# Up products of the ConvFFN: row block outside, column groups inside

## The chip, the cores and the metric

One core of a Trainium2 chip runs the whole program. The metric is device microseconds of one launch, from the first to the last of its work; a number is the median of several runs unless it is said to come from the profiled execution. TensorE is written PE in the rows (its weight loads PEld), VectorE is DVE, ScalarE is ACT, GpSimd is POOL and the queue that issues most transfers is SP.

## The reference, cut to what matters

The kernel does one step of a two-layer decoder for 1024 prompt rows and 64 sample rows. Each layer has a token mixer and a memory attention in parallel, an output projection, and then a gated feed-forward with a causal width-3 convolution. Only the last part concerns the change:

```python
def conv_ffn(x, gain, w_up, cw, cb, w_down, past_rows):
    T = x.shape[1]
    up = rms_norm(x, gain) @ w_up
    ext = jnp.concatenate([past_rows, up], axis=1)
    conv = cb + sum(cw[j] * ext[:, j:j + T] for j in range(CONV_W))
    out = (jax.nn.silu(conv[..., :D_FF]) * conv[..., D_FF:]) @ w_down
    return out, ext[:, ext.shape[1] - (CONV_W - 1):]
```

D_MODEL is 1024, D_FF is 2816, so `w_up` is 1024 x 5632 and `w_down` 2816 x 1024, for each of two layers.

## The kernel before, in words

Every float32 operand of a large product is held as two parts, a high and a low one (`ff_hi`, `ff_lo` for the activations, `w_hi`, `w_lo` for the weights), and a product is three matmuls into the same PSUM tile: high by high, high by low, low by high. The helper `mm3` issues them at lines 360, 361 and 362, so the rows of the profile carry these three lines wherever a product is made; `mm2` (lines 369 and 370) does the same with two matmuls for the 64 sample rows. One call of `matmul` shows as two records, a weight load of the stationary operand and the matmul that streams the moving one.

The feed-forward of a layer is 22 units, one for each 128 columns of the up projection's first half together with the 128 columns of its gate half. `pe_up` makes the up products of unit u. It has two halves (h = 0 and h = 1). In each, the stationary operand is a 128 x 128 block of `w_hi` or `w_lo`, one for each of 8 row blocks k (KT = 8), and the moving operand is a group of token columns of `ff_hi` or `ff_lo`: three groups of 368, 368 and 352 columns (`TG`, numbered g = 0, 1, 2), each with a PSUM bank of its own: banks 0 to 2 for h = 0, banks 3 to 5 for h = 1. The groups stand outside and the row blocks inside, so 24 matmuls in a row go to one bank. For h = 0 the order of groups is 2, 0, 1, for h = 1 it is 0, 1, 2.

`pe_down` then makes the down products of the unit before (u - 1): 18 outputs of up to 128 x 512, numbered q, that rotate over the banks 6, 7, 0, 1 (`DN_BANK`). VectorE adds each to the residual (`dve_adds`, line 2108 for the prompt rows, lines 2112 and 2116 for the sample rows) and counts them on the semaphore `dn_ev`. Banks 0 and 1 are thus used by the up products and by the down products in turn. Before the up products of u may write banks 0 and 1, the additions up to q = 15 of unit u - 2 must be done; that is the wait on `dn_ev` in `pe_up`, which stands ahead of group 0 and therefore behind the 24 matmuls of group 2 (bank 2 is no bank of `DN_BANK`). The first two units of a layer have nothing to wait for there.

ScalarE waits for a whole half (`up_mm`, then `w_used`) and then empties its three banks; VectorE does the convolution taps, the gate and the split of the gated values. The last unit of a layer (`pe_last`) makes its second half's groups one after the other and tells ScalarE after the second of them (`up_part`). It also makes the down products of two units together; there the moving operands are `d_hi`, `d_lo` and, for the second of them, `d_hi_l`, `d_lo_l` elsewhere in memory.

TensorE works through its program in order: up(0), up(1), down(0), up(2), down(1), and so on.

Of the kernel before, what the change touches and what calls it, by code (L numbers as in the profile page):

```python
# [26 lines left out]
P = 128  # L27
D = 1024
KT = D // P
# [21 lines left out]
TG = [368, 368, 352]  # L51
T0 = [0, 368, 736]
CB = 3
DC = 4
# [15 lines left out]
def build(nc, A, O, scratch):  # L70
    es = ExitStack()
    with es:
# [3 lines left out]
        def sb_at(name, shape, off, dt=F32):  # L76
            return nc.alloc_sbuf_tensor_at(name, shape, dt, offset=off)

        def size(shape):
            n = 4  # L80
            for s in shape[1:]:
                n *= s
            return (n + 31) // 32 * 32

        def sb(name, shape, dt=F32):
            t = sb_at(name, shape, place[0], dt)
            place[0] += size(shape)
            return t
# [20 lines left out]
        ff_hi = sb_at("ff_hi", [P, KT, NTOK + NS], act_hi_at, F32R)  # L109
        ff_lo = sb_at("ff_lo", [P, KT, NTOK], act_hi_at + size([P, KT, NTOK + NS]), F32R)  # L110
        w_hi_at = place[0]
        w_hi = sb("w_hi", [P, 2, KT, UW], F32R)
        w_lo = sb("w_lo", [P, 2, KT, UW], F32R)
# [153 lines left out]
        ps = es.enter_context(nc.psum_tensor("ps", [P, 8, 512], F32))  # L267

        def sem(name):
            return es.enter_context(nc.semaphore(name))  # L270
# [30 lines left out]
        up_mm, up_ev, cv_ok, silu_ok, gate_ok, gh_ok, g_ok, dr_ld, dh_ok, d_ok, dn_mm, dn_ev = (  # L301
            sem(n) for n in ("up_mm", "up_ev", "cv_ok", "silu_ok", "gate_ok", "gh_ok", "g_ok", "dr_ld",
                             "dh_ok", "d_ok", "dn_mm", "dn_ev"))
# [4 lines left out]
        tap_ok, up_part, part_ev, part_ok, part_g, part_h, part_lo = (  # L308
            sem(n) for n in ("tap_ok", "up_part", "part_ev", "part_ok", "part_g", "part_h", "part_lo"))
# [48 lines left out]
        def mm3(pe, out, ahi, alo, bhi, blo, first, last, **kw):  # L358

            pe.matmul(out, ahi, bhi, start=first, stop=False, **kw)  # L360
            pe.matmul(out, ahi, blo, start=False, stop=False, **kw)  # L361
            return pe.matmul(out, alo, bhi, start=False, stop=last, **kw)  # L362
# [1533 lines left out]
        def wpar(l, par):  # L1896
            return (ffn0[l] + par) % 2

        def pe_up(pe, l, u, par, last=False):
            n = u + ffn0[l]  # L1900
            U = u + NFT * l
            pe.wait_ge(w_ok, n + 1)
            w = wpar(l, par)
            for h in range(2):
                if not (isinstance(u, int) and u == 0):

                    pe.wait_ge(up_ev, U * 2 + (h - 1))
                for g in ((0, 1, 2) if h else (2, 0, 1)):
                    if h == 0 and g == 0 and not (isinstance(u, int) and u < 2):

                        pe.wait_ge(dn_ev, U * 18 + (DC + 16 - 36))
                    for k in range(KT):
                        cols = slice(T0[g], T0[g] + TG[g])
                        mm = mm3(pe, ps[:, 3 * h + g, 0:TG[g]], w_hi[:, w, k, h * P:(h + 1) * P],
                                   w_lo[:, w, k, h * P:(h + 1) * P], ff_hi[:, k, cols], ff_lo[:, k, cols], k == 0, k == KT - 1)
                    if last and h == 1 and g == 1:
                        mm.then_inc(up_part, 1)
                mm.then_inc(w_used if h else up_mm, 1)

        DN_BANK = [6, 7, 0, 1]  # L1920

# [18 lines left out]

        def pe_last(pe, l, u, par):
            pe_up(pe, l, u, par, True)
            V = u - 1 + NFT * l
            dn0 = DC + V * 18
# [37 lines left out]
        def pe_ffn(pe, l):  # L1982
            pe.wait_ge(pad_ok, 2 * (l + 1))
            def body(u, par):
                pe_up(pe, l, u, par)
                pe_down(pe, l, u - 1, 1 - par)
            ffn_units(pe, l, lambda: pe_up(pe, l, 0, 0), body, lambda u, par: pe_last(pe, l, u, par))
# [506 lines left out]
```

## Time and profile before

| what | value |
|---|---|
| median of 3 runs | 2978.85 us (2978.21 to 2980.59) |
| the profiled execution | 2976.86 us |
| its span, first to last instruction | 2975.2 us |
| mean granted TensorE clock | 0.987 |
| TensorE matmuls, and weight loads | 22376 each |
| of these, up products of the feed-forward | 6336 (3 x 2112) |

The span is what the rows of the profile divide; the 1.7 us between it and the execution's time lie around it. The feed-forward of the first layer begins at 443 us of the span and that of the second at 2183 us. Start times in a timeline are in us from the span's start; a matmul's end is modelled in the profile, so the distance between two starts tells more of its cost than its length does.

### The profile page before, as it was taken

The numbers are of one execution on the slowest core, as the hardware profiler recorded it, in microseconds if no ns is written. First come the engines' busy times: TensorE is split into PE (matmuls) and PEld (weight loads), VectorE is DVE, ScalarE is ACT, GpSimd is POOL, SyncE is SP. The second block draws the span as 40 slices with busy tenths as digits, with TensorE's granted clock in tenths as the row PEclk, the third lists the DMA queues.
The fourth block names the chain that finished last, engine by engine and source line by source line (L and its number), as shares of the span: only waits on it lengthen the run. The fifth ranks groups of instructions, "written<-read, shape, count | busy, mean of one in ns | idle before, by whom it ended". The sixth has DMA issues, their size and how long they took to land.

```text
span 2975.2 us, 55654 instructions
## 1 busy us (share of the span) xinstructions
PE 2851.6 (96%) x22376; PEld 2590.3 (87%) x22376; DVE 1752.5 (59%) x2686; ACT 1103.9 (37%) x2058; POOL 90.2 (3%) x154
## 2 busy tenths in 40 slices
PE   6999999999999999899998988899999999999999
PEld 6998899999999999899995666667999999999998
DVE  4324345767777777633116666774247777777776
ACT  5362243223222223534226666664142222222322
POOL 0000000000000000000110000000000000000000
PEclk9999999999999999999998999999999999999999
DMA  4121211111111111232446666766111111111112
GB/s 142 56 65 65 87 29 47 52 42 42 42 42 42 42 42 43 102 100 88 145 132 233 235 228 221 235 225 207 43 36 43 42 42 42 42 42 42 42 49 73
DMA packets 190181, 265.92 MB, mean 89 GB/s; under 512 B 9704, under 2 KB 138238, under 8 KB 190028
## 3 DMA queue, kind: packets, MB, share of 16 engines
q1 hardware_dynamic: 164464, 197.75, 20.5%
q0 software_dynamic: 16224, 57.26, 6.1%
q10 hardware_dynamic: 9340, 8.66, 0.9%
q8 instruction: 122, 2.00, 0.3%
q14 instruction: 31, 0.25, 0.0%
HBM read 235.95 MB, written 27.68 MB: 89 GB/s over the span
## 4 chain that ended last, share of the span: by engine, by line
PE 87%; DVE 6%; ACT 4%; issue 1%; DMA 1%; ACTq 0%; DVEq 0%; SPq 0%
PE ps L360 24%; PE ps L362 23%; PE ps L361 23%; PE ps L485 2%; DVE left L1563 2%; PE ps L1243 2%; PE ps L1255 2%; PE ps L1341 2%; PE ps L1315 2%; PE ps L369 1%; PE ps L370 1%; ACT bp_s L1451 1%; PE ps L1287 1%; DVE bp_s L1565 1%; PE ps L1323 1%
## 5 line engine op out<-in xcount | busy, mean ns | idle before, releaser
L360 PE MATMUL ps<-ff_hi,w_hi 128*128 128x368 f32 (+1 forms) x2112 | 692.7, 328 | 1.6 <-DVE ff_lo L522 1.6
L362 PE MATMUL ps<-ff_hi,w_lo 128*128 128x368 f32 (+1 forms) x2112 | 692.0, 328 | 0.0
L361 PE MATMUL ps<-ff_lo,w_hi 128*128 128x368 f32 (+1 forms) x2112 | 691.7, 328 | 0.0
L2108 DVE TENSOR_TENSOR x<-x,ps 128x512 f32<-128x512 f32 x640 | 436.3, 688 | 249.1 <-PE ps L362 248.6
L360 PE MATMUL ps<-w_hi,act_hi 128*128 128x256 f32 x1600 | 459.2, 287 | 6.1 <-ACT v_all L721 1.7
L362 PE MATMUL ps<-w_hi,act_lo 128*128 128x256 f32 x1600 | 452.6, 283 | 0.0
L361 PE MATMUL ps<-w_lo,act_hi 128*128 128x256 f32 x1600 | 452.3, 283 | 0.0
L360 PEld LDWEIGHTS ps<-ff_hi,w_hi 128*128 128x128 f32 x2112 | 397.9, 188 | 3.5 <-DVE ff_lo L522 1.9
L361 PEld LDWEIGHTS ps<-ff_lo,w_hi 128*128 128x128 f32 x2112 | 398.0, 188 | 1.5
L362 PEld LDWEIGHTS ps<-ff_hi,w_lo 128*128 128x128 f32 x2112 | 397.8, 188 | 0.0
L360 PEld LDWEIGHTS ps<-w_hi,act_hi 128*128 128x128 f32 x1600 | 303.9, 190 | 16.9 <-issue 10.0
L361 PEld LDWEIGHTS ps<-w_lo,act_hi 128*128 128x128 f32 x1600 | 304.7, 190 | 0.0
L362 PEld LDWEIGHTS ps<-w_hi,act_lo 128*128 128x128 f32 x1600 | 304.4, 190 | 0.0
L2068 ACT ACTIVATE g_hi<-cv_u 128x1088 fp32r<-128x1088 f32 x42 | 46.8, 1115 | 624.9 <-DVE cv_u L2134 624.9
L360 PE MATMUL ps<-d_hi,g_hi 128*128 128x512 f32 x672 | 263.0, 391 | 0.0
L362 PE MATMUL ps<-d_hi,g_lo 128*128 128x512 f32 x672 | 262.2, 390 | 0.0
L361 PE MATMUL ps<-d_lo,g_hi 128*128 128x512 f32 x672 | 261.5, 389 | 0.0
L356 DVE TENSOR_TENSOR w_lo<-w_raw,w_hi 128x2048 fp32r<-128x2048 f32 x73 | 167.3, 2291 | 61.7 <-ACT w_hi L352 61.7
L352 ACT ACTIVATE w_hi<-w_raw 128x2048 fp32r<-128x2048 f32 x73 | 139.1, 1906 | 149.9 <-PE ps L370 136.1
L2038 ACT ACTIVATE up_g<-ps 128x736 f32<-128x736 f32 x44 | 34.7, 788 | 394.1 <-PE ps L362 394.1
L362 PEld LDWEIGHTS ps<-d_hi,g_lo 128*128 128x128 f32 x672 | 126.1, 188 | 27.4
L361 PEld LDWEIGHTS ps<-d_lo,g_hi 128*128 128x128 f32 x672 | 126.2, 188 | 25.2
(338 smaller groups left out, 3992.0 us busy)
## 6 DMA issues: line engine op xcount, KB each, us to landing
pk_raw<-in_cache_sb_k_dram SPq DMA_DIRECT2D x128, 384.0 KB, 4.5
w_raw<-in_w_up_dram SPq DMA_DIRECT2D x88, 512.0 KB, 5.1
d_raw<-in_w_down_dram POOLq DMA_DIRECT2D x44, 512.0 KB, 3.5
pv_hi<-in_cache_sb_v_dram SPq DMA_DIRECT2D x32, 384.0 KB, 4.4
pv_lo<-in_cache_sb_v_dram SPq DMA_DIRECT2D x32, 384.0 KB, 4.7
pv_raw<-in_cache_sb_v_dram SPq DMA_DIRECT2D x32, 384.0 KB, 4.9
pv_own<-in_cache_sb_v_dram SPq DMA_DIRECT2D x32, 384.0 KB, 5.0
w_raw<-in_w_in_b_dram SPq DMA_DIRECT2D x20, 512.0 KB, 4.8
```

Of the source, the lines that this page charges most:

```text
L352: act.activation(w_hi[:, par], w_raw[:, :, :], ACT.Copy).then_inc(wh_ok, 1)
L356: dve.tensor_tensor(w_lo[:, par], w_raw[:, :, :], w_hi[:, par].bitcast(F32), ALU.subtract).then_inc(w_ok, 1)
L360: pe.matmul(out, ahi, bhi, start=first, stop=False, **kw)
L361: pe.matmul(out, ahi, blo, start=False, stop=False, **kw)
L362: return pe.matmul(out, alo, bhi, start=False, stop=last, **kw)
L485: last = pe.matmul(out, src(t, k), diag[0:ROWS[t], t, 0:ROWS[t]], start=True, stop=True, skip_group_check=True)
L1243: last = pe.transpose(ps[:, bank, (2 * u + j) * P:(2 * u + j + 1) * P], pk_raw[:, 2 * (G % 2) + j, a * P:(a + 1) * P], ident[:, :])
L1255: last = pe.matmul(ps[32 * j:32 * j + 32, 5, 0:2 * P], qb[:, b, 2 * j + r, :], k_t[:, 2 * j + r, :], start=(r == 0), stop=(r == 1), skip_g ...
L1315: pe.matmul(ps[:, 3 + h, 0:n], q_t[rows, t * P:(t + 1) * P], kk_t[rows, k0:k0 + n], start=True, stop=True).then_inc(bp_z, 1)
L1341: last = pe.matmul(ps[rows, 7, (t % 4) * P:(t % 4 + 1) * P], sb_v[i % 2][:, k0 + j, rows], bp_at[:, (W_BEFORE[u] + c) % 2, h, j * P:(j + 1 ...
L1563: dve.tensor_tensor_scan(c[:, ::-1], c[:, ::-1], zi[:, SEQ - w:SEQ][:, ::-1], 0.0, ALU.mult, ALU.add).then_inc(bp_left, 1)
L2108: dve.tensor_tensor(xs, xs, ps[:, DN_BANK[(2 * t + c) % 4], :], ALU.add).then_inc(dn_ev, 1)
```

## The change

The three column groups move inside the row block. For each row block k and each of the three kinds of product (high weights by high activations, high weights by low activations, low weights by high activations) the matmuls of all three groups are issued one after the other with the same stationary operand. Three in a row share `w_lo`'s block, six in a row share `w_hi`'s block. Consecutive matmuls then go to three banks in turn. Each output still sums the same 24 products in the same order. Since banks 0 and 1 are now written from the start, the wait on `dn_ev` goes ahead of the whole first half. The second half of a layer's last unit keeps its old order.

```diff
-                for g in ((0, 1, 2) if h else (2, 0, 1)):
-                    if h == 0 and g == 0 and not (isinstance(u, int) and u < 2):
-
-                        pe.wait_ge(dn_ev, U * 18 + (DC + 16 - 36))
-                    for k in range(KT):
+                if h == 0 and not (isinstance(u, int) and u < 2):
+
+                    pe.wait_ge(dn_ev, U * 18 + (DC + 16 - 36))
+                if last and h:
+                    for g in range(3):
                         cols = slice(T0[g], T0[g] + TG[g])
-                        mm = mm3(pe, ps[:, 3 * h + g, 0:TG[g]], w_hi[:, w, k, h * P:(h + 1) * P],
-                                   w_lo[:, w, k, h * P:(h + 1) * P], ff_hi[:, k, cols], ff_lo[:, k, cols], k == 0, k == KT - 1)
-                    if last and h == 1 and g == 1:
-                        mm.then_inc(up_part, 1)
+                        for k in range(KT):
+                            mm = mm3(pe, ps[:, 3 * h + g, 0:TG[g]], w_hi[:, w, k, h * P:(h + 1) * P],
+                                     w_lo[:, w, k, h * P:(h + 1) * P], ff_hi[:, k, cols], ff_lo[:, k, cols], k == 0, k == KT - 1)
+                        if g == 1:
+                            mm.then_inc(up_part, 1)
+                else:
+                    mm = pe_up_half(pe, w, h)
                 mm.then_inc(w_used if h else up_mm, 1)
+
+        def pe_up_half(pe, w, h):
+            for k in range(KT):
+                wh, wl = w_hi[:, w, k, h * P:(h + 1) * P], w_lo[:, w, k, h * P:(h + 1) * P]
+                for n, (lhs, src) in enumerate(((wh, ff_hi), (wh, ff_lo), (wl, ff_hi))):
+                    for g in ((0, 1, 2) if h else (2, 0, 1)):
+                        mm = pe.matmul(ps[:, 3 * h + g, 0:TG[g]], lhs, src[:, k, T0[g]:T0[g] + TG[g]],
+                                       start=(k == 0 and n == 0), stop=(k == KT - 1 and n == 2))
+            return mm
```

## Rows read from the trace of the kernel before

**Rows 1.** The page's first part: busy time of each engine, share, instructions.

```profile
PE 2851.6 (96%) x22376; PEld 2590.3 (87%) x22376; DVE 1752.5 (59%) x2686; ACT 1103.9 (37%) x2058; POOL 90.2 (3%) x154
```

**Rows 2.** The chain that ended last, share of the span by engine.

```profile
PE 87%; DVE 6%; ACT 4%; issue 1%; DMA 1%; ACTq 0%; DVEq 0%; SPq 0%
```

**Rows 3.** Costliest groups: busy us, mean ns of one, idle before and its releaser.

```profile
L360 PE MATMUL ps<-ff_hi,w_hi 128*128 128x368 f32 (+1 forms) x2112 | 692.7, 328 | 1.6 <-DVE ff_lo L522 1.6
L362 PE MATMUL ps<-ff_hi,w_lo 128*128 128x368 f32 (+1 forms) x2112 | 692.0, 328 | 0.0
L361 PE MATMUL ps<-ff_lo,w_hi 128*128 128x368 f32 (+1 forms) x2112 | 691.7, 328 | 0.0
...
L360 PEld LDWEIGHTS ps<-ff_hi,w_hi 128*128 128x128 f32 x2112 | 397.9, 188 | 3.5 <-DVE ff_lo L522 1.9
L361 PEld LDWEIGHTS ps<-ff_lo,w_hi 128*128 128x128 f32 x2112 | 398.0, 188 | 1.5
```

**Rows 4.** Windows: us; busy by engine (instructions); then granted clock, DMA share, GB/s.

```profile
1108.00:1144.00 36.00, 36.00 (x200) 33.85 (x199) 26.45 (x41) 10.06 (x14) 0.53 (x1) 1.00 0.15 44
...
2182.80:2187.50 4.70, 4.68 (x16) 4.70 (x17) 2.29 (x1) 1.35 (x1) 0.00 (x0) 0.50 0.00 0
```

**Rows 5.** Timeline of PE through one unit: start us, length us, instruction.

```profile
1108.31 0.39 PE L370 MATMUL ps<-d_lo,g_hi 128*128 128x512 f32 x1
1108.54 0.32 PE L360 MATMUL ps<-ff_hi,w_hi 128*128 128x352 f32 x1
...
1112.34 0.33 PE L360 MATMUL ps<-ff_hi,w_hi 128*128 128x368 f32 x1
...
1113.02 0.33 PE L361 MATMUL ps<-ff_lo,w_hi 128*128 128x368 f32 x1
...
1116.35 0.33 PE L360 MATMUL ps<-ff_hi,w_hi 128*128 128x368 f32 x1
...
1120.40 0.33 PE L360 MATMUL ps<-ff_hi,w_hi 128*128 128x368 f32 x1
...
1144.09 0.32 PE L360 MATMUL ps<-ff_hi,w_hi 128*128 128x352 f32 x1
```

**Rows 6.** Timeline of PE, the down products after that unit's up products.

```profile
1132.25 0.40 PE L360 MATMUL ps<-d_hi,g_hi 128*128 128x512 f32 x1
...
1134.57 0.39 PE L361 MATMUL ps<-d_lo,g_hi 128*128 128x512 f32 x1
...
1135.02 0.39 PE L360 MATMUL ps<-d_hi,g_hi 128*128 128x512 f32 x1
1135.25 0.39 PE L361 MATMUL ps<-d_lo,g_hi 128*128 128x512 f32 x1
...
1136.84 0.39 PE L362 MATMUL ps<-d_hi,g_lo 128*128 128x512 f32 x1
```

**Rows 7.** Timeline of the weight loads at the start of the same unit.

```profile
1108.54 0.19 PEld L361 LDWEIGHTS ps<-ff_lo,w_hi 128*128 128x128 f32 x1
```

**Rows 8.** Timeline of DVE at the start of the same unit.

```profile
1106.47 2.05 DVE L2108 TENSOR_TENSOR x<-x,ps 128x512 f32<-128x512 f32 x3
```

**Rows 9.** Timelines of DVE and PE, a wait inside the first layer's last unit.

```profile
1207.74 0.92 DVE L2183 TENSOR_TENSOR g_lo<-cv_u,g_hi 128x736 fp32r<-128x736 f32 x1
...
1208.72 0.50 PE L360 MATMUL ps<-d_hi_l,g_hi 128*128 128x512 f32 x1 [0.39 <-DVE g_lo L2183]
1209.05 0.40 PE L361 MATMUL ps<-d_lo_l,g_hi 128*128 128x512 f32 x1
```

**Rows 10.** Timeline of PE in that last unit, d and d_l by turns.

```profile
1220.04 0.39 PE L360 MATMUL ps<-d_hi,g_hi 128*128 128x512 f32 x1
...
1222.83 0.39 PE L360 MATMUL ps<-d_hi,g_hi 128*128 128x512 f32 x1
```

**Rows 11.** Timeline of PE, the first layer's first unit, 352 columns.

```profile
443.37 0.33 PE L361 MATMUL ps<-ff_lo,w_hi 128*128 128x352 f32 x1
...
444.20 0.35 PE L360 MATMUL ps<-ff_hi,w_hi 128*128 128x352 f32 x1
```

## The prediction

> **What bounds the kernel now.** I read the page from the top. TensorE is busy 96% of the span, VectorE 59%, and TensorE has exactly as many weight loads as matmuls, 22376 [rows 1]. The chain of waits says that this is no average that hides another bound: 87% of the chain that ended last is TensorE's [rows 2]. The costliest groups are the up products, three lines of 2112 matmuls, with 1.6 us of idle time in all [rows 3]. The windows over one unit of the feed-forward show TensorE busy in 36.00 of 36.00 us at a granted clock of 1.00 [rows 4], so inside the 40 repeating units nothing hides anything that TensorE does longer, and each ns saved or lost per matmul comes out at the end.
>
> What one matmul costs is the distance between starts. A unit takes 1144.09 - 1108.54 = 35.55 us [rows 5]: its up products from 1108.54 to 1132.25, 23.71 us [rows 5, 6], the rest its down products. Blocks of 24: group 2 takes 1112.34 - 1108.54 = 3.80 us, 158.3 ns each; group 0 takes 4.01 us, 167.1 each; group 1 takes 4.05 us, 168.8 each [rows 5]. At 2.4 GHz, the level that a granted clock of 1.00 stands for, 352 columns stream in 146.7 ns and 368 in 153.3, so each matmul pays 12 to 15 ns beyond its columns. At the level of 1.2 GHz sixteen matmuls of 352 columns take 4.70 us, 293.8 each [rows 4], which is the columns alone (293.3): there the excess is hidden, so it isn't the loading itself.
>
> **What the change does to the loads.** Lines 360 and 361 already share a stationary operand (`w_hi`), and both have all 2112 loads of 188 ns [rows 3]: nothing skips a repeated load. The load for line 361 starts at 1108.54, together with the matmul ahead of it [rows 7, 5], and so lies under it. Nor is a matmul with repeated weights quicker: in settled down products the two steps from 1134.57 to 1135.02 both bring new weights (the second a new bank as well) and take 0.45 us, 0.225 each, and the step to 1135.25, with the same weights as before it, takes 0.23 [rows 6]. So I price "sharing" at nothing: same loads, same matmuls, same columns. What covers the loads is the matmul ahead, 158 ns or more.
>
> The Trainium skill, "TensorE: Matmul & The Clock Gate", section "Part 2: What happens when you issue a matmul", says that weights can be loaded once for many matmuls, and that the next load is pulled ahead of a running matmul. The second half agrees with the row of the 1108.54 load; the first doesn't happen here, where a repeated operand is loaded again 2112 times. By the gap that the same page gives for a stream without loads (columns at 2.4 GHz plus 2.5 ns; an estimate) the up products whose weights repeat would lose about 11 ns each, some 53 us in all, before the wait below; by the rows, nothing.
>
> **The moved wait.** Before, the wait for the additions up to q = 15 stood behind the 3.80 us of group 2, and so cost nothing. Now it stands ahead of the first up matmul, with up_ev and w_ok, which are long satisfied. The addition of q = 15 is the last of three that end at 1106.47 + 2.05 = 1108.52 [rows 8], and the first up matmul starts at 1108.54, its load having started with the matmul ahead, at 1108.31 [rows 5]. So the wait now ends after that load should have started. What a late wait costs is shown once: the split of g_lo ended at 1207.74 + 0.92 = 1208.66, the waiting matmul starts at 1208.72, and its successor 0.33 us later instead of 0.23, since its own load was no longer covered [rows 9]. Effective start: 0.06 + 0.10 = 0.16 us after the release. Here that is 1108.68 instead of 1108.54, 0.14 us. Behind it queue the unit's 144 up matmuls, ScalarE's evacuation and the next down products; all shift alike, and the additions follow TensorE's down products, so the lag comes back in each unit. Units 2 to 21 of two layers have it: 40 x 0.14 = 5.7 us. Nothing gives it back. The bounds are 0 (if the load were not held) and 40 x 0.22 = 8.8 us (if none of the old lead counted and another 0.06 us of sequencer time came on top).
>
> **The pitch of interleaved groups.** The trace has no stream that changes its column group and its bank at each matmul, so this has two bounds. The change counts 2 x 44 x 24 = 2112 triples (one matmul of each group) less the 48 of the two last halves, 2064. Now a triple costs 23.71 / 48 = 494.0 ns, of which 1088 / 2.4 = 453.3 are columns. Lower bound: each pays only group 2's excess, 158.3 - 146.7 = 11.7 ns: 488.4, so 2064 x -5.6 = -11.6 us. Upper bound: each pays what the stream that alternates between d and d_l pays, twelve matmuls in 1222.83 - 1220.04 = 2.79 us, 232.5 each [rows 10], 19.2 over the 213.3 of 512 columns: 510.9, so +34.9 us. Between lie the switches that there are. After the switch from 352 to 368 columns the first four matmuls take 1113.02 - 1112.34 = 0.68 us where the block's other twenty take 0.666 per four (3.33 / 20): +14 ns [rows 5]. The switch from 352 to 512 costs more, the first ten taking 2.32 us and the next ten 2.27 [rows 6]. The block of group 1, same width as before it, shows no such start. So a stream needs a few matmuls to settle after its width changes, and the new order changes width twice per triple and never settles. I take a quarter of the 14 ns, 3 ns per triple, as nearest: one switch from 352 to 368 in each triple, cut off after its first matmul. 2064 x 3 = 6.2 us.
>
> **Sum.** 5.7 + 6.2 = 11.9 us on the profiled 2976.86 us (span 2975.2 and 1.7 around it): 2988.8. The median of the runs shown lies 2.0 above that execution, so for a median I predict 2990.8 us, 0.4% slower. ScalarE and VectorE are left as they were: evacuation waited for a whole half before too, and no transfer moves.
>
> **The rivals.**
>
> *Only the wait.* Each matmul keeps its excess, because it belongs to the operand's place and not to the neighbour; the blocks' different but repeating pitches (158.3, 166.7, 168.8) speak for that. Then +0 to +8.8 us, in the middle 5.7: 2984.6, which is within 0.2% of before (6.0 us, about what a measurement of this kernel can tell from no change). It holds if the pitch effect is under 0.3 us in 6000 matmuls, and that is narrow.
>
> *Never settled.* The interleaved stream pays the upper bound, 34.9 + 5.7 = 40.6 us: 3019.4. For it: alternating streams do so [rows 10]; and after a late start 352 columns took (444.20 - 443.37) / 5 = 166 ns instead of 158 [rows 11], and now each unit starts late. Against it: groups 0 and 1 pass into each other without loss.
>
> *Settling at the best pitch, faster.* Three banks in turn could take away a turn-round in one bank and give all matmuls 11.7 ns of excess: -11.6 + 5.7 = -5.9, or -11.6 if the wait is hidden: 2967 to 2973. It ends on the faster side only when the groups of 368 come under 165.5 ns and the stall under 0.14 us. Against it: the settled down products change bank after every third matmul, the step to 1135.02 among them, and it shows no price or gain [rows 6].
>
> *Loads dropped.* If six or three equal loads in a row were run once, 14 of 18 matmuls would lose their excess of 13.6 ns: 0.78 x 6192 x 13.6 = 65 us, less the wait: about 2919. Against it speaks line 361, which would show it already. This would be the case in which the change does what it says.
>
> **How the numbers follow.** Chances: forecast (wait and some pitch, +6 to +22 us) 0.45; never settled 0.18; only the wait or less, within 0.2%, 0.27; best pitch 0.07; loads dropped 0.03. Faster 0.10, same 0.27, slower 0.63. The range that leaves out less than 2 in 10 starts above the best-pitch case and takes in nearly all of the never-settled one: 2974 to 3017. The forecast's own range, 0.45 of the chance, is 2985 to 3001.
>
> **What the profile after would show.** Right: 22376 loads still; in the units a start-to-start gap of some 0.37 us between the last down matmul and the first up matmul or its successor, in 40 places, with VectorE's line 2108 as releaser, about 3 us or more of idle in that group; a triple of starts at 497 ns; unit pitch 35.55 + 0.14 + 0.14 = 35.84 us. Wrong: a triple at 494 or under (only the wait, or best pitch); at 505 or more (never settled); fewer loads, or loads that vanish for repeated weights; no gap at the unit's start, which would mean that the load went ahead of the wait.

## The result and the profile after

The changed kernel takes 2988.89 us (median of 6 runs, 2986.93 to 2990.78), the kernel before 2978.64 (6 runs): a ratio of 1.0033, 95% interval 1.0022 to 1.0043. That is 10 us more, clear of the 6 us under which the prediction would have called it no change (the interval is 6.6 to 12.8 us), and 2 us from the 2990.8 predicted.

The page of the profiled execution (2986.93 us), its span, the engines' busy time, the chain's shares by engine, and the groups that took the place of [rows 3]:

```profile
span 2985.3 us, 55654 instructions
...
PE 2859.2 (96%) x22376; PEld 2590.1 (87%) x22376; DVE 1752.3 (59%) x2686; ACT 1103.8 (37%) x2058; POOL 90.2 (3%) x154
...
PE 87%; DVE 6%; ACT 4%; issue 1%; DMA 1%; ACTq 0%; SPq 0%; DVEq 0%
...
L1928 PE MATMUL ps<-ff_hi,w_hi 128*128 128x352 f32 (+1 forms) x2064 | 458.2, 330 | 1.6 <-DVE ff_lo L522 1.6
...
L1928 PEld LDWEIGHTS ps<-ff_hi,w_hi 128*128 128x128 f32 x2064 | 354.4, 188 | 13.8 <-DVE x L2120 11.2
L1928 PEld LDWEIGHTS ps<-ff_hi,w_lo 128*128 128x128 f32 x2064 | 356.3, 188 | 0.0
```

There are 22376 weight loads, as before [rows 1], though six and three in a row now name the same operand, and each still takes 188 ns. The other engines are busy for the same time. The group's PE row names no new idle time, only its load row does: 11.2 us before loads, released by VectorE's additions (line 2120 is line 2108 of before); the prediction had asked for about 3 us or more. The modelled ends of matmuls cover gaps of this size, so the load's row is the one to look at.

The timelines of PE and PEld at the start of a unit, of VectorE there, and of PE at the seventh and the last triple of that unit and at the next unit; "x3" stands for three matmuls in a row, one for each group:

```profile
1112.60 0.39 PE L370 MATMUL ps<-d_lo,g_hi 128*128 128x512 f32 x1
1112.86 0.75 PE L1928 MATMUL ps<-ff_hi,w_hi 128*128 128x352 f32 x3
...
1112.86 0.46 PEld L1928 LDWEIGHTS ps<-ff_hi,w_hi 128*128 128x128 f32 x3 [0.29 <-DVE x L2120]
...
1110.08 2.73 DVE L2120 TENSOR_TENSOR x<-x,ps 128x512 f32<-128x512 f32 x4
...
1115.94 0.66 PE L1928 MATMUL ps<-ff_hi,w_hi 128*128 128x352 f32 x3
...
1136.31 0.66 PE L1928 MATMUL ps<-ff_hi,w_lo 128*128 128x368 f32 x3
...
1148.65 0.76 PE L1928 MATMUL ps<-ff_hi,w_hi 128*128 128x352 f32 x3
```

The addition of q = 15 ends at 1110.08 + 2.73 = 1112.81, and the load of the first up matmul starts at 1112.86, together with its matmul. Before, that load started with the matmul ahead of it, at 1108.31 [rows 5]; its row in the timeline of PEld before:

```profile
1108.31 0.19 PEld L360 LDWEIGHTS ps<-ff_hi,w_hi 128*128 128x128 f32 x1
```

From the triple at 1115.94 to the one at 1136.31 lie 41 triples in 20.37 us, 496.8 ns each, against 494.0 before; 497 was predicted. The unit takes 1148.65 - 1112.86 = 35.79 us against 35.55 [rows 5]; 35.84 was predicted. Forty units of 0.24 us are 9.6 of the 10.1 us by which the span grew (2985.3 - 2975.2). That the rest is so small is chance: from the first layer's last unit to the second layer's first the trace has 1003.2 us before and 1006.1 after, in the second layer's first two units 62.0 and 59.6, and both vary from run to run whatever the order (the version in blocks of 384, 384 and 320 columns, below, has 1007.1 and 59.3).

### The profile page after: what moved, and what is told of

It is laid out like the page before. It is cut to its first block, busy times and chain, and to the rows that moved or that the text cites. A ratio compares the mean times of both kernels' runs of the same rounds, so it can differ in the third digit from the quotient of the medians.

```text
span 2985.3 us, 55654 instructions
## 1 busy us (share of the span) xinstructions
PE 2859.2 (96%) x22376; PEld 2590.1 (87%) x22376; DVE 1752.3 (59%) x2686; ACT 1103.8 (37%) x2058; POOL 90.2 (3%) x154
## 4 chain that ended last, share of the span: by engine, by line
PE 87%; DVE 6%; ACT 4%; issue 1%; DMA 1%; ACTq 0%; SPq 0%; DVEq 0%
PE ps L1928 35%; PE ps L360 12%; PE ps L362 12%; PE ps L361 12%; PE ps L485 2%; DVE left L1563 2%; PE ps L1243 2%; PE ps L1341 2%; PE ps L1255 2%; PE ps L1315 2%; PE ps L369 1%; PE ps L370 1%; ACT bp_s L1451 1%; DVE bp_s L1565 1%; PE ps L1287 1%
## 5 line engine op out<-in xcount | busy, mean ns | idle before, releaser
L1928 PE MATMUL ps<-ff_hi,w_hi 128*128 128x352 f32 (+1 forms) x2064 | 458.2, 330 | 1.6 <-DVE ff_lo L522 1.6
L1928 PE MATMUL ps<-ff_hi,w_lo 128*128 128x352 f32 (+1 forms) x2064 | 454.0, 328 | 0.0
L1928 PE MATMUL ps<-ff_lo,w_hi 128*128 128x352 f32 (+1 forms) x2064 | 453.9, 328 | 0.0
L1928 PEld LDWEIGHTS ps<-ff_hi,w_hi 128*128 128x128 f32 x2064 | 354.4, 188 | 13.8 <-DVE x L2120 11.2
L1928 PEld LDWEIGHTS ps<-ff_hi,w_lo 128*128 128x128 f32 x2064 | 356.3, 188 | 0.0
L1928 PEld LDWEIGHTS ps<-ff_lo,w_hi 128*128 128x128 f32 x2064 | 356.1, 188 | 0.0
L360 PEld LDWEIGHTS ps<-d_hi,g_hi 128*128 128x128 f32 x672 | 126.2, 188 | 25.1
```

The source lines that it names most:

```text
L1928: mm = pe.matmul(ps[:, 3 * h + g, 0:TG[g]], lhs, src[:, k, T0[g]:T0[g] + TG[g]], start=(k == 0 and n == 0), stop=(k == KT - 1 and n == 2))
```

## The experiments

Each diff is against the kernel that the text names, cut to the lines that matter; "..." marks a cut. The theory at this point: two separate prices, the late start of each unit and a longer pitch of interleaved matmuls; repeated weights are worth nothing.

**Only the wait moved.** From the kernel before, groups outside as ever:

```diff
+                if h == 0 and not (isinstance(u, int) and u < 2):
+                    pe.wait_ge(dn_ev, U * 18 + (DC + 16 - 36))
                 for g in ((0, 1, 2) if h else (2, 0, 1)):
-                    if h == 0 and g == 0 and not (isinstance(u, int) and u < 2):
-                        pe.wait_ge(dn_ev, U * 18 + (DC + 16 - 36))
```

> Groups stay outside as before; only the wait for the additions goes ahead of the first half. Theory (the wait and the interleaved pitch are two separate prices): each of 40 units starts 0.14 us late, the blocks of 24 keep their 3.80, 4.01 and 4.05 us; +5.7 us, some 2984.5. Rival A (the late start also unsettles the stream, and that is all of the loss): the pitch within the blocks rises too and the time is near that of the changed kernel, +9 to +10 us. Rival B (interleaving alone is the loss): no gap at the unit's start, within 1 us of before.

Measured: 2986.07 us, ratio 1.0021 (1.0012 to 1.0031). PE's timeline at the start of a unit and of the next:

```profile
1112.40 0.39 PE L370 MATMUL ps<-d_lo,g_hi 128*128 128x512 f32 x1
1112.66 0.43 PE L360 MATMUL ps<-ff_hi,w_hi 128*128 128x352 f32 x1
1112.93 0.32 PE L361 MATMUL ps<-ff_lo,w_hi 128*128 128x352 f32 x1
...
1148.36 0.43 PE L360 MATMUL ps<-ff_hi,w_hi 128*128 128x352 f32 x1
```

Two steps take 0.53 us that took 1108.70 - 1108.31 = 0.39 in the same view before: 0.14 us, in two parts, a later matmul and a longer way to its successor. The unit takes 35.70 us, 0.15 more than before. 40 x 0.15 is 6.0 us, which the interval (3.6 to 9.2 us) holds. The wait alone is thus a good half of the loss, and rival B falls.

**The wait covered.** From the changed kernel; group 2's three products of the first row block go ahead of the wait:

```diff
...
-                for n, (lhs, src) in enumerate(((wh, ff_hi), (wh, ff_lo), (wl, ff_hi))):
-                    for g in ((0, 1, 2) if h else (2, 0, 1)):
+                three = list(enumerate(((wh, ff_hi), (wh, ff_lo), (wl, ff_hi))))
+                groups = (0, 1, 2) if h else (2, 0, 1)
+                todo = [(n, lhs, src, g) for n, (lhs, src) in three for g in groups]
+                if h == 0 and k == 0:
+                    todo.sort(key=lambda t: t[3] != 2)
+                for i, (n, lhs, src, g) in enumerate(todo):
+                    if waits and k == 0 and i == 3:
+                        pe.wait_ge(dn_ev, U * 18 + (DC + 16 - 36))
...
```

> The changed order, but the first row block's three products of group 2 go ahead of the wait, 0.48 us of cover for 0.14 us. Theory: no gap at the unit's start, a triple of matmuls still at 496.6 ns instead of 494.0; +4 to +5 us over before, 5.7 under the changed kernel. Rival A: the pitch goes back to 494 with the stall, and the time is that of before. Rival B: as slow as the changed kernel.

Measured: 2983.39 us, ratio 1.0014 (1.0005 to 1.0023). PE's timeline at the unit's start, over seven later triples, at the first down product, and at the next unit:

```profile
1111.94 0.39 PE L370 MATMUL ps<-d_lo,g_hi 128*128 128x512 f32 x1
1112.16 0.32 PE L1931 MATMUL ps<-ff_hi,w_hi 128*128 128x352 f32 x1
1112.32 0.32 PE L1931 MATMUL ps<-ff_lo,w_hi 128*128 128x352 f32 x1
...
1118.12 0.66 PE L1931 MATMUL ps<-ff_hi,w_hi 128*128 128x352 f32 x3
...
1121.60 0.66 PE L1931 MATMUL ps<-ff_lo,w_hi 128*128 128x352 f32 x3
...
1136.00 0.39 PE L360 MATMUL ps<-d_hi,g_hi 128*128 128x512 f32 x1
...
1147.81 0.32 PE L1931 MATMUL ps<-ff_hi,w_hi 128*128 128x352 f32 x1
```

The start is as before the change (0.22 and 0.16 us), the seven triples take 3.48 us, 497 ns each. The unit takes 35.65 us, 0.10 over before: the up products are 0.13 us longer (1136.00 - 1112.16 = 23.84 against 23.71), the down products some 0.03 shorter (11.81 against 1144.09 - 1132.25 = 11.84 [rows 5, 6]). 40 x 0.10 = 4.0 us, within the interval (1.5 to 6.9). With the wait's 0.15 this makes up the 0.24 of the changed kernel to 0.01 us, so the prices add; rival A falls.

**Only the second half interleaved.** From the changed kernel, the first half as before, with the wait in its old place:

```diff
...
-                if last and h:
-                    for g in range(3):
+                if last and h or h == 0:
+                    for g in ((0, 1, 2) if h else (2, 0, 1)):
+                        if h == 0 and g == 0 and not (isinstance(u, int) and u < 2):
+                            pe.wait_ge(dn_ev, U * 18 + (DC + 16 - 36))
...
```

> The first half keeps the old order and the old place of the wait; only the second half is interleaved. Theory: no gap, the second half's 24 triples at 496.6 ns, +0.06 us per unit, +2.5 us in all. Rival A: 494 ns, time as before. Rival C (a change of order costs a fixed price per half, not per triple): the second half longer by the same 0.06 but with all of it in its first matmuls.

Measured: 2980.95 us, ratio 1.0009 (1.0000 to 1.0018). PE's timeline at the second half's start, twelve triples on, and at the first down product:

```profile
1121.46 0.66 PE L1928 MATMUL ps<-ff_hi,w_hi 128*128 128x368 f32 x3
...
1127.41 0.66 PE L1928 MATMUL ps<-ff_hi,w_hi 128*128 128x368 f32 x3
...
1133.38 0.40 PE L360 MATMUL ps<-d_hi,g_hi 128*128 128x512 f32 x1
```

24 triples take 11.92 us, 496.7 ns each, against 1132.25 - 1120.40 = 11.85 in blocks [rows 5, 6]. Half the interleaving, half the pitch's price, without any wait. The two dozens of triples take 5.95 and 5.97 us, so the price lies on every triple and not on the first ones: rival C falls.

**No two matmuls in a row with the same weights.** From the changed kernel; row blocks k and k + 1 by turns, everything else alike:

```diff
-            for k in range(KT):
+            for k in range(0, KT, 2):
...
-                    for g in ((0, 1, 2) if h else (2, 0, 1)):
-                        mm = pe.matmul(ps[:, 3 * h + g, 0:TG[g]], lhs, src[:, k, T0[g]:T0[g] + TG[g]],
+                    for i in range(6):
+                        g, j = groups[i % 3], i % 2
+                        mm = pe.matmul(ps[:, 3 * h + g, 0:TG[g]], lhs[j], src[:, k + j, T0[g]:T0[g] + TG[g]],
...
```

> The changed order of groups (another bank and column group at each matmul, wait ahead), but the row blocks go in pairs by turns, so that no two matmuls in a row have the same stationary operand. Each output sums the same 24 products, two row blocks by turns. Theory (every matmul loads its weights under the matmul ahead, whether they repeat or not): triple at 496.6 ns and 2988.9 us, as the changed kernel. Rival D (repeated weights do save something, and the interleaved groups cost more than it seems): triple above 500 ns, over 2996 us.

Measured: 2989.22 us, ratio 1.0035 (1.0021 to 1.0049). PE's timeline, "x6" being two triples:

```profile
1118.05 1.16 PE L1931 MATMUL ps<-ff_lo,w_hi 128*128 128x352 f32 x6
...
1122.02 0.49 PE L1931 MATMUL ps<-ff_hi,w_lo 128*128 128x352 f32 x2
```

Eight triples in 3.97 us, 496 ns each: the same pitch and the same time as the changed kernel, though no two weights in a row are the same. That the weights repeat is worth nothing; rival D falls.

What remained was the pitch: is it the change of bank, of width or of place from matmul to matmul? "Place" means the column at which a group starts within a row block of `ff_hi` or `ff_lo`.

**One place, three banks.** From the changed kernel, all three groups read group 2's columns.

```diff
-                        mm = pe.matmul(ps[:, 3 * h + g, 0:TG[g]], lhs, src[:, k, T0[g]:T0[g] + TG[g]],
+                        mm = pe.matmul(ps[:, 3 * h + g, 0:TG[2]], lhs, src[:, k, T0[2]:T0[2] + TG[2]],
...
```

> The changed order, but all three groups read the same 352 columns, those of group 2 (the up products of the other columns are left out; 16 columns of two banks keep old contents). Banks still rotate at each matmul and weights still repeat, while width and place of the moving operand no longer change. Theory (the price of interleaving, 2.6 ns per triple, comes with the moving operand's width or place, not with the bank): 158.3 ns per matmul, 475.0 per triple, as in group 2's own block before. Rival E (the rotating bank is the price): 159.2 ns, 477.5 per triple.

PE's timeline, ten triples apart:

```profile
1097.00 0.64 PE L1928 MATMUL ps<-ff_hi,w_hi 128*128 128x352 f32 x3
...
1101.75 0.64 PE L1928 MATMUL ps<-ff_lo,w_hi 128*128 128x352 f32 x3
```

4.75 us for ten triples: 475 ns, 158.3 per matmul, as group 2's own block [rows 5]. With one width and one place, changing the bank at each matmul costs nothing and gives nothing. Nor does it matter here that three matmuls in a row read the same columns of the same tile, where in blocks the moving operand goes from `ff_hi` to `ff_lo` or to the next row block at every matmul. (One run each for this and the next two, 2943.64, 2963.76 and 2949.02 us; work is left out, so only the pitch is read.)

**One width, three places, interleaved and in blocks.** From the changed kernel and from the kernel before; each group 352 columns at its own place (the diff is that of the first; the second has the same widths and places in its `mm3` call).

```diff
-                        mm = pe.matmul(ps[:, 3 * h + g, 0:TG[g]], lhs, src[:, k, T0[g]:T0[g] + TG[g]],
+                        mm = pe.matmul(ps[:, 3 * h + g, 0:TG[2]], lhs, src[:, k, T0[g]:T0[g] + TG[2]],
...
```

> The changed order, three groups of 352 columns at their three places 0, 368 and 736 (the last 16 columns of the first two groups are left out). To be read against the same columns in blocks. If the width is the price, both have the same triple; if the place is, this one is 2 to 3 ns longer. Guess: the width, so no difference, within 0.5 ns.

> The order of before, groups of 352 columns at the places 0, 368 and 736 (the last 16 columns of the first two groups are left out). If a group's excess over its columns belongs to its place, the blocks are 146.7 + 13.3 = 160.0 ns for group 0, 146.7 + 15.5 = 162.2 for group 1 and 158.3 for group 2, 480.5 per triple. If it belongs to the width, all three are 158.3 and a triple 475.0.

PE's timeline, interleaved, six triples apart:

```profile
1118.41 0.64 PE L1928 MATMUL ps<-ff_hi,w_lo 128*128 128x352 f32 x3
...
1121.31 0.64 PE L1928 MATMUL ps<-ff_hi,w_lo 128*128 128x352 f32 x3
```

and in blocks, at the start of group 2, of group 0 and four matmuls on, of group 1 and of the second half:

```profile
1094.88 0.32 PE L360 MATMUL ps<-ff_hi,w_hi 128*128 128x352 f32 x1
...
1098.68 0.33 PE L360 MATMUL ps<-ff_hi,w_hi 128*128 128x352 f32 x1
...
1099.32 0.32 PE L361 MATMUL ps<-ff_lo,w_hi 128*128 128x352 f32 x1
...
1102.52 0.32 PE L360 MATMUL ps<-ff_hi,w_hi 128*128 128x352 f32 x1
...
1106.36 0.32 PE L360 MATMUL ps<-ff_hi,w_hi 128*128 128x352 f32 x1
```

Interleaved: 2.90 us for six triples, 483 ns. In blocks: 11.48 us for 24, 478; the blocks take 3.80, 3.84 and 3.84 us, 158.3, 160.0 and 160.0 ns per matmul. So at one width the interleaving still costs some 5 ns per triple, and my guess that it was the width is wrong. The places matter, in blocks too (158.3 or 160.0), though by less than the 162.2 expected for group 1.

**One start, two widths.** The kernel with only the second half interleaved, all groups reading from column 720 on, in both halves.

```diff
-                        cols = slice(T0[g], T0[g] + TG[g])
+                        cols = slice(720, 720 + TG[g])
...
-                        mm = pe.matmul(ps[:, 3 * h + g, 0:TG[g]], lhs, src[:, k, T0[g]:T0[g] + TG[g]],
+                        mm = pe.matmul(ps[:, 3 * h + g, 0:TG[g]], lhs, src[:, k, 720:720 + TG[g]],
...
```

> Groups of 368, 368 and 352 columns that all start at column 720 (what is computed from the other columns is left out); the first half in blocks, the second half interleaved, so the width changes within a triple and the start doesn't. Place theory: the second half's triple equals the sum of the first half's three blocks per matmul, within 0.5 ns. Width rival (the prediction's own reason): 2 to 3 ns longer.

PE's timeline at the unit's start, at the switch to 368 columns and four matmuls on, at the second half and at the first down product:

```profile
1107.90 0.32 PE L360 MATMUL ps<-ff_hi,w_hi 128*128 128x352 f32 x1
...
1111.74 0.33 PE L360 MATMUL ps<-ff_hi,w_hi 128*128 128x368 f32 x1
...
1112.41 0.33 PE L361 MATMUL ps<-ff_lo,w_hi 128*128 128x368 f32 x1
...
1119.74 0.66 PE L1928 MATMUL ps<-ff_hi,w_hi 128*128 128x368 f32 x3
...
1131.59 0.39 PE L360 MATMUL ps<-d_hi,g_hi 128*128 128x512 f32 x1
```

11.84 us in blocks, 11.85 interleaved (2974.39 us, one run). Two widths by turns from one start cost nothing: the width rival falls, and the price comes only where the place changes. Every version that pays it changes the bank along with the place; a change of place within one bank was not run.

**Other widths and places.** The groups 384, 384 and 320 columns wide, at 0, 384 and 768; first the kernel before, then the one with only its second half interleaved:

```diff
-TG = [368, 368, 352]
-T0 = [0, 368, 736]
+TG = [384, 384, 320]
+T0 = [0, 384, 768]
```

> The order of before with groups of 384, 384 and 320 columns in place of 368, 368 and 352: the same work, other widths and places. If each pays 13.3 ns over its columns, 173.3, 173.3 and 146.7, a triple is 493.3 and the time 1.5 us under before, not to be told from it; if all places pay as little as group 2 does now (11.7), 488.4 and 12 us under before; if as much as group 1 (15.5), 499.8 and 12 us over.

> Groups of 384, 384 and 320 columns at the places 0, 384 and 768 (all the work is done); the first half in blocks as before, the second half interleaved. In blocks these cost 173, 173 and 147 ns, 493 per triple. Theory F (each change of the moving operand's place costs something, whatever the places): second half 495 to 498 per triple, time 1 us over the same groups in blocks. Theory G (it depends on which places follow each other): 493, and time as the same groups in blocks, 2977.

In blocks: 2976.92 us, ratio 0.9991 (0.9982 to 1.0000), as expected of 493 ns per triple and hardly to be told from before. Half interleaved: 2981.85 us, ratio 1.0017 (1.0008 to 1.0026). PE's timeline of the latter, at the two halves and the first down product:

```profile
1111.22 0.30 PE L360 MATMUL ps<-ff_hi,w_hi 128*128 128x320 f32 x1
...
1123.05 0.65 PE L1928 MATMUL ps<-ff_hi,w_hi 128*128 128x384 f32 x3
...
1135.04 0.40 PE L360 MATMUL ps<-d_hi,g_hi 128*128 128x512 f32 x1
```

11.83 us in blocks, 11.99 interleaved: 492.9 and 499.6 ns per triple. Theory F's sign holds and its size doesn't: 6.7 ns, against 2.7 at the places of the changed kernel. Here widths and places both differ from those of the changed kernel. The places alone don't set the price either: at 0, 368 and 736 it is 2.7 ns with groups of 368, 368 and 352 columns and some 5 with three of 352. How width and place set it together, no run here shows.

## Why the prediction was right

**Loads.** "Same loads, same matmuls, same columns" held: as many loads after as before, and the version without repeated operands has the same pitch and time. The rival with dropped loads, and with it the reading that a shared operand is loaded once, is out.

**The wait.** The price taken from the one late wait that the trace had [rows 9] was 0.14 us a unit; the version with only the wait moved shows 0.14 at the unit's start and 0.15 per unit, and covering it with three matmuls gives it back. It shows as two longer steps, 0.26 for 0.23 and 0.27 for 0.16 us, and not as the single one of 0.37 that the prediction looked for. The step that mattered was to set the end of the addition beside the start of the load and not of the matmul: 1108.52 [rows 8] is ahead of the matmul's 1108.54 and yet too late for its load at 1108.31. Of the 40 places, 38 have the addition as releaser in the changed kernel; the two last units have a late start too, which the profile puts down to nothing it shows (in the first layer's, the addition ends at 1184.39 us and the load starts at 1184.50).

**The pitch.** 3 ns per triple was forecast and 2.7 measured, but the reason given with it was wrong. "A stream needs a few matmuls to settle after its width changes" is not what costs: one start with two widths is free, one width with three places is not. The switch from 352 to 368 columns in [rows 5] was also a switch of place, and I read the half of it that I could see in the row. Its 14 ns don't belong to either half alone: the first four matmuls after a switch take 1099.32 - 1098.68 = 0.64 us where only the place changes, as four at 160.0 ns do, and 1112.41 - 1111.74 = 0.67 where only the width does, as at the 166.7 ns of those two blocks (8.00 us for 48). That a quarter of the 14 ns came out near the price is luck, as the groups of 384, 384 and 320 columns show, where the same order costs 6.7 ns. The prediction also had no term for the down products, which take some 0.03 us a unit less behind these interleaved groups.

**The rivals.** "Only the wait" underrated the loss by the 0.10 us per unit that stay when the wait is covered. "Never settled" asked for 505 ns or more per triple; 497 came. "Best pitch" needs a gain from rotating the banks, and there is none.

## What to carry to other kernels

Sharing a stationary operand between neighbouring matmuls paid nothing here, because no load fell away and the loads lay under the matmuls ahead of them. Before making such a change, look in the trace for two matmuls that share an operand already, count their loads and compare their steps. When a wait moves ahead of a matmul, compare the releaser's end with the start of that matmul's load: a release some 0.02 us ahead of the matmul's own start still cost 0.14 us in each unit here, and three independent matmuls ahead of the wait were enough to hide it. On an engine that is never idle, order alone moves the time: in the three layouts measured with different places, runs of 24 matmuls from one start column were cheaper than a new start column at each matmul.

## What the runs showed that was not expected

The distance between matmuls of one width depends on where the moving operand starts: 352 columns took 158.3 ns from column 736 and 160.0 from columns 0, 368 and 720; 368 columns took 167.1 and 168.8 from columns 0 and 368 (the 167.1 hold the 14 ns of that block's start; its other twenty matmuls took 166.5 each). Interleaving such streams costs more than the sum of the parts by 2.7 to 6.7 ns per triple in the three layouts with different places, and nothing in the two that share a start.
